# The second feed-forward block starts with a four-tile product scheme, and all its kind take their seven products in another order

## The reference

```python
x = x + 0.5 * swiglu(rms_norm(x, ffn1_norm), ffn1_w_gate, ffn1_w_up, ffn1_w_down)
h = rms_norm(x, mix_norm)
...
x = x + jnp.concatenate([y_ssd, y_pool], axis=-1) @ w_out
x = x + 0.5 * swiglu(rms_norm(x, ffn2_norm), ffn2_w_gate, ffn2_w_up, ffn2_w_down)
return rms_norm(x, final_norm)
# swiglu(h, g, u, d) = (silu(h @ g) * (h @ u)) @ d, width 2816 = 22 tiles of 128
```

## Time and profile before

| what | value |
|---|---|
| median of 3 executions | 985.36 us (984.82 to 986.02) |
| profiled execution, its own time | 984.7 us |
| its span | 982.9 us |
| TensorE matmul busy | 973.9 us (99%) |
| VectorE busy | 755.4 us (77%) |
| ScalarE busy | 481.0 us (49%) |
| GpSimd busy | 204.0 us (21%) |
| granted TensorE clock, mean | 0.999 of full |
| bytes read from HBM | 102.30 MB, 106 GB/s over the span |

### The profile page before, as it was taken

The page is one execution under the profiler, slowest core; times in us unless marked ns, Lnnn a source line. Parts: engine busy times, 40 slices in busy tenths (PEclk is TensorE's granted clock), DMA queues, the critical chain, the costliest instruction groups (busy, mean ns, idle before and its releaser), DMA issues.

```text
span 982.9 us, 15859 instructions
## 1 busy us (share of the span) xinstructions
PE 973.9 (99%) x6353; PEld 874.8 (89%) x6353; DVE 755.4 (77%) x921; ACT 481.0 (49%) x670; POOL 204.0 (21%) x172
## 2 busy tenths in 40 slices
PE   9999999999999999999999999999999999999997
PEld 8999889998999878878788888899988999889986
DVE  6888478985698788765579796798956899568964
ACT  6655235552355556564445653555532555325543
POOL 1012002220032222222063461201300223002321
PEclk9999999999999999999999999999999999999999
DMA  9525304552143343434443132263451335413412
GB/s 270 150 62 159 112 24 119 139 151 86 42 112 86 86 128 87 133 97 117 144 139 100 58 93 86 78 159 87 134 153 58 87 102 153 132 43 87 118 34 86
DMA packets 192368, 105.46 MB, mean 107 GB/s; under 512 B 4100, under 2 KB 189608, under 8 KB 192296
## 3 DMA queue, kind: packets, MB, share of 16 engines
q1 hardware_dynamic: 191624, 103.40, 37.7%
q10 hardware_dynamic: 672, 1.05, 0.3%
HBM read 102.30 MB, written 2.13 MB: 106 GB/s over the span
## 4 chain that ended last, share of the span: by engine, by line
PE 97%; DVE 1%; ACT 1%; issue 1%; DVEq 0%; POOL 0%; POOLq 0%
PE bank L1704 12%; PE bank L1702 12%; PE bank L1703 12%; PE bank L1617 8%; PE bank L1619 8%; PE bank L1618 8%; PE bank L1722 8%; PE bank L1721 8%; PE bank L1720 8%; PE bank L1625 7%; PE bank L1863 1%; PE bank L1870 1%; PE bank L1850 0%; PE bank L1760 0%; PE bank L1963 0%
## 5 line engine op out<-in xcount | busy, mean ns | idle before, releaser
L612 POOL TENSOR_TENSOR post<-post,rstd 128x256 f32<-128x256 f32 x57 | 93.1, 1633 | 514.9 <-DVE post L1143 514.9
L1703 PE MATMUL bank<-tlo,w_hi_part 128*128 128x256 f32 x608 | 167.8, 276 | 0.0
L1704 PE MATMUL bank<-thi,w_lo_part 128*128 128x256 f32 x608 | 167.8, 276 | 0.0
L1702 PE MATMUL bank<-thi,w_hi_part 128*128 128x256 f32 x608 | 167.8, 276 | 0.0
L1053 DVE TENSOR_TENSOR w_lo_part<-w_raw,w_hi_part 128x1024 fp32r<-128x1024 f32 (+1 forms) x102 | 129.8, 1273 | 18.4 <-ACT w_hi_part L700 16.1
L1720 PE MATMUL bank<-acthi,w_hi_part 128*128 128x512 f32 x340 | 132.7, 390 | 0.0
L1722 PE MATMUL bank<-acthi,w_lo_part 128*128 128x512 f32 x340 | 132.3, 389 | 0.0
L1721 PE MATMUL bank<-actlo,w_hi_part 128*128 128x512 f32 x340 | 132.3, 389 | 0.0
L1702 PE MATMUL bank<-xfhi,w_hi_part 128*128 128x256 f32 x418 | 115.6, 277 | 0.0
L1703 PE MATMUL bank<-xflo,w_hi_part 128*128 128x256 f32 x418 | 115.5, 276 | 0.0
L709 ACT ACTIVATE w_hi_part<-w_raw 128x1024 fp32r<-128x1024 f32 x76 | 80.3, 1057 | 71.8 <-PE bank L1704 36.8
(11 more groups left out here) (287 smaller groups left out, 2107.8 us busy)
## 6 DMA issues: line engine op xcount, KB each, us to landing
w_raw<-in_ffn_w_gate SPq DMA_DIRECT2D x42, 512.0 KB, 4.1
w_raw<-in_ffn_w_up SPq DMA_DIRECT2D x42, 512.0 KB, 5.3
w_raw<-in_ffn_w_down SPq DMA_DIRECT2D x32, 512.0 KB, 5.2
w_raw<-in_w_in SPq DMA_DIRECT2D x29, 512.0 KB, 3.9
w_raw<-in_w_out SPq DMA_DIRECT2D x16, 512.0 KB, 3.8
w_raw<-in_ffn_w_down SPq DMA_DIRECT2D x16, 384.0 KB, 4.2
decay<-acs_rows SPq DMA_DIRECT2D x16, 256.0 KB, 4.5
out<-xtok SPq DMA_DIRECT2D x4, 512.0 KB, 2.6
```

The costliest lines, as they stand in the source:

```text
L1702: pe.matmul(out, w, hi, start=opens and e == 0 and k == 0, stop=False, skip_group_check=True)
L1703: pe.matmul(out, w, lo, start=False, stop=False, skip_group_check=True)
L1704: mm = pe.matmul(out, wl, hi, start=False, stop=end, skip_group_check=True)
```

## The change

The second block has no direct tiles any more: its first group is four quads (tiles 0 to 7). In every quad of both blocks the order of the products becomes A11, A12, SUM2, SUM1, SUM3, SUM4, A22. The output projection takes its tiles in the order 0, 4, 1, 5, 2, 6, 3, 7, so that a pair j, j + 4 is complete after every second unit. The first two weight sums of the first quad are made in the sixth and seventh projection step, the third behind the eighth. `stat(2)` moves behind the second product, `rms(2)` and `inverse(2)` into the block.

```diff
-DIRECT_TILES = (4, 2)
+DIRECT_TILES = (4, 0)
...
-A11, SUM1, SUM2, A12, SUM3, SUM4, A22 = range(PARTS)
+A11, A12, SUM2, SUM1, SUM3, SUM4, A22 = range(PARTS)
...
+OUT_ORDER = (0, 4, 1, 5, 2, 6, 3, 7)
# SyncE
-            for i in range(DK):
-                mix_fetch(U_OUTS + i, w_out[:, 0:DK, block(i)])
+            for i, d in enumerate(OUT_ORDER):
+                mix_fetch(U_OUTS + i, w_out[:, 0:DK, block(d)])
# ScalarE, in ffn
-                    if it.kind == "product" and it.part == SUM1:
+                    if it.kind == "product" and it.part == A12:
                         copy_product(q, A11, 0, q % 2, p1_read, act0_ready)
-                    if it.kind == "product" and it.part == SUM2:
+                    if it.kind == "product" and it.part == SUM3:
                         copy_product(q, SUM1, 1, 2, p5_read, act22_ready)
-                    if it.kind == "product" and it.part == A12:
+                    if it.kind == "product" and it.part == SUM1:
                         copy_product(q, SUM2, 2, q % 2, u2_read, act0_ready)
...
-                    if f and it.kind == "direct" and it.raw == 0:
-                        combination_hi(1, KH - 1)
+                    if f and r == 2:
+                        rms(2)
# ScalarE, output projection
-            for d in range(DK):
-                norm_hi(2, d, R_N2)
-                if d >= KH:
-                    halves_of_x(1, d - KH, R_N2)
-                square(2, d, d % 2, xT[:, cols(d)])
-                convert(M + U_OUTS + d + RING)
-                if d > KH:
-                    combination_hi(1, d - KH - 1)
-            rms(2)
+            for i, d in enumerate(OUT_ORDER):
+                if i % 2 == 0:
+                    halves_of_x(1, d, R_N2)
+                norm_hi(2, d, R_N2, seen=i)
+                if i == DK - 1:
+                    combination_hi(1, KH - 1)
+                square(2, i, i % 2, xT[:, cols(d)])
+                convert(M + U_OUTS + i + RING)
+                if i % 2 and i < DK - 1:
+                    combination_hi(1, i // 2)
# VectorE, in ffn
-                    if product and it.part == SUM1:
+                    if product and it.part == SUM2:
                         fourth_sum(q)
...
-                    if f and it.kind == "direct" and it.raw:
-                        combine_low(1, it.raw)
+                    if f and r == 4:
+                        inverse(2)
# VectorE, output projection
-            for d in range(DK):
-                dve.wait_ge(unit_done, d + (M + U_OUTS + 1))
-                dve.tensor_tensor(xT[:, cols(d)], PB[4 + d % 2][:, :], xT[:, cols(d)], ALU.add).then_inc(x_ready, 1)
-                if d == KH + 1:
+            first = DIRECT_QUADS
+            for i, d in enumerate(OUT_ORDER):
+                dve.wait_ge(unit_done, i + (M + U_OUTS + 1))
+                dve.tensor_tensor(xT[:, cols(d)], PB[4 + i % 2][:, :], xT[:, cols(d)], ALU.add).then_inc(x_ready, 1)
+                if i == 1:
                     dve.wait_ge(neg_ready, 2)
-                if d > KH:
-                    combine(1, d - KH - 1, R_N2)
-                norm_lo(2, d, R_N2)
-                convert(M + U_OUTS + d + RING)
-            combine(1, KH - 1, R_N2)
-            combine_low(1, 0)
-            inverse(2)
+                if i == 5:
+                    first_sum(first)
+                if i == 6:
+                    second_sum(first)
+                if i == DK - 1:
+                    norm_lo(2, d, R_N2, seen=i)
+                if i % 2:
+                    dve.wait_ge(x_ready, i + (2 * DK + 1))
+                    combine(1, i // 2, R_N2)
+                elif i:
+                    combine_low(1, i // 2 - 1)
+                if i < DK - 1:
+                    norm_lo(2, d, R_N2, seen=i)
+                    convert(M + U_OUTS + i + RING)
+            combine_low(1, KH - 1)
+            convert(M_FFN2 + SUM1)
+            third_sum(first)
# TensorE, in product
+                if n == M_FFN2:
+                    pe.wait_ge(xg_lo, 3 * DK - 1)
+                if f and local == 0 and part == A12:
+                    pe.wait_ge(xg_lo, 3 * DK)
+                order = [(e, k) for e in range(2) for k in range(KH)]
+                if f and local == 0 and part == SUM2:
+                    order = [(e, k) for k in range(KH) for e in range(2)]
...
-                        if n == M_FFN2:
-                            stat(2)
                     if it.kind == "product":
                         product(f, it, n)
+                        if n == M_FFN2 + A12:
+                            stat(2)
```

More of the change, by code:

```diff
@@ L713, in convert, with norm_hi @@
                     act.activation(whi[:, slot(n), 0:blocks], raw[:, it.raw % RAW, 0:blocks], ACT.Copy).then_inc(w_hi, 1)
-            def norm_hi(p, d, gain):
-                act.wait_ge(x_ready, d + (DK * p + 1))
+            def norm_hi(p, d, gain, seen=None):
+                act.wait_ge(x_ready, (d if seen is None else seen) + (DK * p + 1))
                 act.activation(normed(p)[0][d], xT[:, cols(d)], ACT.Copy,
@@ L740, in halves_of_x @@
             def halves_of_x(f, j, gain):
-                act.wait_ge(x_ready, DK * 2 * f + j + 1)
+                act.wait_ge(x_ready, DK * 2 * f + (1 + f) * j + 1)
                 act.activation(b12[:, j, :], xT[:, j * S + HALF:(j + 1) * S], ACT.Copy,
@@ L788, in ffn @@
                     chained = it.kind == "product" and QUADS[q].chained
+                    if it.kind == "product" and it.part == A12:
+                        copy_product(q, A11, 0, q % 2, p1_read, act0_ready)
+                    if it.kind == "product" and it.part == SUM3:
+                        copy_product(q, SUM1, 1, 2, p5_read, act22_ready)
                     if it.kind == "product" and it.part == SUM1:
-                        copy_product(q, A11, 0, q % 2, p1_read, act0_ready)
-                    if it.kind == "product" and it.part == SUM2:
-                        copy_product(q, SUM1, 1, 2, p5_read, act22_ready)
-                    if it.kind == "product" and it.part == A12:
                         copy_product(q, SUM2, 2, q % 2, u2_read, act0_ready)
-                    if chained and it.part == SUM1:
+                    if chained and it.part == A12:
                         silu_odd(q - 1)
@@ L1054, in convert, with norm_lo @@
                                       whi[:, slot(n), 0:blocks].bitcast(F32), ALU.subtract).then_inc(w_lo, 1)
-            def norm_lo(p, d, gain):
-                dve.wait_ge(xg_hi, d + (DK * p + 1))
+            def norm_lo(p, d, gain, seen=None):
+                dve.wait_ge(xg_hi, (d if seen is None else seen) + (DK * p + 1))
                 dve.scalar_tensor_tensor(out=normed(p)[1][d], in0=xT[:, cols(d)], scalar=par[:, one(d + gain)],
@@ L1245, in ffn @@
                         act_low(f, QUADS[q - 1].tile, 0)
+                    if chained and it.part == SUM1:
                         act21(q - 1)
-                    if chained and it.part == A12:
                         act22(q - 1)
@@ L1651, in direct @@
                     pe.wait_ge((g_scaled, act_ready)[it.part], tile - 1)
-                from_x(PB[bank], n, *normed(2 * f), ready=(xg_lo, 2 * DK) if n == M_FFN2 else None)
+                from_x(PB[bank], n, *normed(2 * f))
             def moving(f, part, k):
@@ L1693, in product @@
                 pe.wait_ge(w_lo, n + 1)
-                for e in range(2):
-                    out = bank[:, half(e)]
[L1696 to L1704, removed]
+                if n == M_FFN2:
[5 more added lines that the diff above has]
+                    order = [(e, k) for k in range(KH) for e in range(2)]
+                for i, (e, k) in enumerate(order):
+                    out = bank[:, half(e)]
+                    if part == SUM2 and local == 0 and e == 0:
+                        pe.wait_ge(t_lo, KH * f + k + 1)
+                    hi, lo = moving(f, part, k)
+                    w, wl = whi[:, slot(n), e * KH + k, :], wlo[:, slot(n), e * KH + k, :]
+                    end = k == KH - 1
+                    pe.matmul(out, w, hi, start=opens and i == 0, stop=False, skip_group_check=True)
+                    pe.matmul(out, w, lo, start=False, stop=False, skip_group_check=True)
+                    mm = pe.matmul(out, wl, hi, start=False, stop=end, skip_group_check=True)
                 mm.then_inc(unit_done, 1)
```

## The result

| | before | changed |
|---|---|---|
| median | 985.26 us (984.23 to 986.02, 16 runs) | 986.94 us (986.04 to 987.98, 16 runs) |
| ratio | | 1.0018, 95% interval 1.0011 to 1.0024 |
| profiled execution: its time, span | 984.7, 982.9 us | 987.8, 986.1 us |

The change costs 1.7 us, 0.2%. The forecast was 987.0 us, 1.7 more than before. Most of its mechanism was right; one rival that had been given 3 in 100, the fall of the clock, took place in the profiled execution beside it.

What follows compares the result with a forecast made beforehand. TensorE was taken to bound the kernel. Waits of 0.4 + 0.55 + 2.5 + 0.75 + 0.2 = 4.4 us against 2.7 us saved gave +1.7 us: 985.36 + 1.7 = 987.0 us, range 984.6 to 989.2.

Steps and rivals of the forecast that it cites:

- What bounds: Whole kernel: TensorE, busy 99% of the span, sets the time; a saving must take matmuls away.
- the saving: Second block's first tiles: four direct units (21.78 us) become seven products (19.08 us), 2.70 us saved.
- T: The end of the last output-projection unit, 636.17 us in the kernel before; later times count from it.
- VectorE late at T: Last projection steps: overruns of 1.0 and 0.46 us; VectorE starts the last addition at about T + 1.4, not T + 0.04.
- The two low-part waits: First two products after T: TensorE waits 0.4 and 0.55 us for low parts of x.
- The statistics: Behind the second product: TensorE waits 2.5 us for GpSimd's sum of squares, the last square standing behind the last `combination_hi`.
- The chain to the second quad: VectorE's work after T: A22 waits 0.75 us, then 0.15 to 0.2 more; second quad at T + 24.4.
- The new order at 0: All quads: reordered products give VectorE 0.55 us of new pause per chained quad, priced at 0.
- Rival 3: Three following quads: VectorE never regains its lead, 0.6 us each, +3.5 us in all, 988.9; chance 0.10.
- rival 4: Around the statistics: clock falls during 2.5 us idle, 3 us at half rate add 1.5: +3.2 us, 988.6; chance 0.03.
- Terms, summed: From T to the second quad: waits of 4.4 us against 2.7 us saved, +1.7 us.
- the bound: Upper side of the waits after T: TensorE restarts and slots of 0.1 us could add 1 us.

Runs made afterwards that it cites:

- e4: Changed kernel with GpSimd adding only 8 of 512 columns of each square in front of the second block: 985.23 us.
- e1: Changed kernel with nine filler matmuls of ones on TensorE in front of the wait for the sum of squares: 986.87 us.
- e2: Changed kernel with ScalarE's last square ahead of the last high part of a combination: 987.20 us.
- e5: Changed kernel with the second weight sum moved into VectorE's pause before the last combine_low, its conversion following: 987.07 us.
- e6: Changed kernel with the last square first and the first bank's copy right behind it, waiting for seven low combinations: 987.03 us.
- e12: Changed kernel with SUM1's conversion in VectorE's pause, the last square first and the first bank's copy early: 985.78 us, ratio 1.0005.
- e9: Changed kernel with the second block's reciprocal over 8 of 512 columns: 987.25 us.
- e10: Changed kernel with the second block's reciprocal over 8 of 512 columns and nine filler matmuls before the statistics: 986.28 us.
- e3: Kernel before with only the order of the seven products changed, in both blocks: 985.23 us, ratio 1.0000.
- e7: Changed kernel with the second block's reciprocal moved two units later on VectorE: 992.29 us.
- e8: Changed kernel with the second weight sum in VectorE's pause and the reciprocal two units later: 993.80 us.
- e11: Changed kernel with SUM1's conversion in VectorE's pause and nine filler matmuls before the statistics: 986.36 us, ratio 1.0011.

## Why the prediction was right, and where it was not

- **What bounds** and **the saving**: 24 matmuls fewer, as forecast. From its first matmul to the next unit's, a product unit measures 2.72 us and a direct one 5.48 (653.33 to 658.81 in the kernel before). I had the 5.48 and took 5.44, from 22.64 us that begin at T, the recorded end of a matmul, 0.16 us behind the first matmul of the stretch. The saving is 4 x 5.48 - 7 x 2.72 = 2.9 us, not 2.7.
- **VectorE late at T**: forecast 1.0 us late after i = 5 and 1.4 us at T. (Its own terms, 0.04 + 1.02 + 0.46, give 1.5.) Measured: 632.63 against 637.13 - 5.44 + 0.04 = 631.73, so 0.90, and 1.22 at T. The cause was shown by e4: without GpSimd's length the lateness is nil. The Trainium skill's rule (SBUF — State Buffer, "SBUF: two separate sides") agrees with both stretched rows, 1.97 us instead of 0.87 and 1.78 instead of 0.75.
- **The two low-part waits**: forecast 0.4 + 0.55, measured 0.30 + 0.28. **The statistics**: forecast 2.5, measured 2.03, in the place and for the reason given; the last square runs at T + 6.14, forecast T + 6.4.
- **The chain to the second quad**: forecast A22 0.75 and 0.2 more, the second quad at T + 24.4. With the clock at full: 0.60 (e1), T + 24.22 to 24.25 in four kernels (e1, e2, e5, e6) whose early waits differ in place. That four such numbers agree within 0.03 us is the best evidence for the step: whatever TensorE waits for first, VectorE's list of work after T ends the same. e12 shortened the list by 1.1 us and the quad came 1.1 us sooner; e9 and e10 took 3.2 us out, and then TensorE's own waits were left.
- **The new order at 0**: e3, 0.0 us; the pause laid out as 0.55 measures 0.57. **Rival 3**, a lead never regained: not in the changed kernel, all later units at 2.72 or 2.76 us.
- **The step that failed: rival 4.** "Idle of 4 us went unpunished here and 2.5 should be" was drawn from one tail. 2.03 us was enough in the profiled execution. Over all profiled executions with this wait the clock fell in two (changed 2.03 us, e7 2.02) and held in three (e5 2.02, e8 2.03, e9 2.11), and by their mean clocks it fell in six of the eleven of e9. An idle stretch that left the clock alone once doesn't say that a shorter one is safe. The Trainium skill (TensorE: Matmul & The Clock Gate, "Part 1: The HAM clock gate") says of the clock's rise, not of its fall, that its point varies between runs of one kernel; no run here bears on the rise, and what varied here is the fall. The 3 us at half rate of the price stood in no row; measured are 3.4 us, and 1.62 us of SUM2. The forecast survived because the chain covered the fall: 24.87 - 24.23 = 0.64 us net instead of the 1.5 us priced.
- **Terms, summed**, with the clock at full: the four waits of the lists, 0.30 + 0.28 + 2.03 + 0.60, delay TensorE by 0.16 us more each, 3.85 us instead of 4.4. What runs right behind a wait takes 0.12 to 0.21 us longer, four times, 0.63 us in all; that I had only in the bound. Together 4.48 against 2.88 saved: +1.6 us, and e1's second quad is 1.59 later than that of the kernel before. The waits were 0.55 us too long, the slower products missing and the saving 0.2 too small. The mechanism is the forecast one, but that its total came within 0.1 us is luck.

## What to carry to other kernels

- When a bound engine's work is cut, list what its suppliers must still do between two fixed points; if that list is as long as the bound stretch, the saved time turns into waits, and moving the waits about gives nothing. A filled pause counts only if nothing is pushed over the fixed point with it.
- Before an operation is moved later, follow every engine's queue behind what waits for its result, not the total of its own engine: a reciprocal of 3.35 us moved by two units cost 5.3 us.
- A wait of TensorE of 2 us was followed by half its clock in some executions and not in others; compare means over many, and test with filler matmuls before blaming the clock for the loss.

## What was not expected of the hardware

- The clock fell after 2.0 to 2.1 us of idleness in some profiled executions and held in others, and e9's mean clocks show both within one kernel; in the changed kernel's profiled one it came back 4.3 us after TensorE had taken up work again.
- A slower pace at a granted clock of 1.00. In some executions product units took 2.83 us instead of 2.72 for 5 to 8 units in a row, without waits: e5 from 698 to 718, e6 from 663 to 683, e11 from 649 to 663. Windows of e5, normal and slow (73 matmuls in 8 us, 138 in 16):

```profile
690.00:698.00 8.00, 8.00 (x73) 8.00 (x72) 8.00 (x9) 4.65 (x6) 3.32 (x2) 1.00 0.70 195
700.00:716.00 16.00, 16.00 (x138) 16.00 (x137) 15.15 (x18) 9.07 (x13) 4.63 (x3) 1.00 0.32 86
```

  It costs 0.5 to 0.9 us, occurs in the profiled executions of e2, e5 to e9 and e11 and not in those of before, changed, e1, e3, e4, e10 and e12. In six of the seven it begins 1 to 6 us behind the end of a wait of TensorE, in e5 40 us behind. It may be what splits the executions of e10 and e11: the profiled one of e11, with the slow pace, is among the 986.3 to 987.0 us and that of e10, without it, among the 985.1 to 985.5. That is not shown, and its cause stays open.
